# Hybrid MLA and sparse attention, two layers: scores ahead of the transposes of a step, a fourth buffer of probabilities, copies and exponentials by turns

## The reference

```python
h = rms_norm(x, attn_norm[l]); proj = h @ w_in[l]
o_mla = mla_attention(...)      # 8 heads, latent q and kv, rope, causal softmax, 4 query blocks of 128
o_nsa = nsa_attention(...)      # 8 heads, 2 kv groups: compressed + selected + window branches, gated
x = x + concat([o_mla, o_nsa]) @ w_out[l]
x = x + conv_ffn(rms_norm(x, ffn_norm[l]), ...)   # up projection, conv of width 3, silu gate, down projection
```

## Time and profile before

| what | value |
|---|---|
| median of 3 runs | 1303.52 us (1303.19 to 1304.73) |
| the profiled execution, own time | 1304.81 us |
| its span | 1303.0 us |
| PE / PEld / DVE / ACT busy over the span | 97% / 80% / 54% / 49% |
| granted TensorE clock, mean | 0.997 |
| share of the chain that ended last: PE / DVE / ACT | 84% / 8% / 6% |
| L1449 to L1451, matmul busy time of the costliest group of each | 298.2, 296.9 and 296.8 us |
| exponentials L860 | 192, 106.1 us busy, 28.5 us waited for `nmax` |
| transposes L1645 | 480, 72.1 us busy |

### The profile page before, as it was taken

One profiled execution on the slowest core, in us unless ns is written; L12 is line 12 of the kernel. 1 busy time (PEld: TensorE's weight loads), 2 busy tenths in 40 slices (PEclk: granted clock), 3 DMA queues, 4 the chain that ended last, 5 costly groups with the idle time before them and its releaser, 6 DMA issues.

```text
span 1303.0 us, 18497 instructions
## 1 busy us (share of the span) xinstructions
PE 1265.0 (97%) x6612; PEld 1045.6 (80%) x6612; DVE 704.0 (54%) x1232; ACT 639.2 (49%) x1193; POOL 71.1 (5%) x157
## 2 busy tenths in 40 slices
PE   8999989999999999999999998999999999999997
PEld 7997667778888888888889876677888888888885
DVE  5435887454555555533363459872555555554334
ACT  4336888344444444322352479881444444443223
POOL 2003020000000000000010311100000000000000
PEclk9999999999999999999999999999999999999999
DMA  6420200123333333332143211002233333333221
GB/s 206 125 90 1 98 34 1 39 73 113 95 93 100 95 93 102 103 97 96 53 122 95 65 66 50 17 1 81 81 85 95 97 97 95 96 101 108 97 64 65
DMA packets 121002, 107.04 MB, mean 82 GB/s; under 512 B 3763, under 2 KB 110485, under 8 KB 120946
## 3 DMA queue, kind: packets, MB, share of 16 engines
q1 hardware_dynamic: 118912, 101.13, 25.3%
q0 software_dynamic: 1456, 3.52, 0.9%
q10 hardware_dynamic: 578, 1.64, 0.3%
HBM read 104.19 MB, written 2.10 MB: 82 GB/s over the span
## 4 chain that ended last, share of the span: by engine, by line
PE 84%; DVE 8%; ACT 6%; issue 2%; DMA 0%; ACTq 0%; DVEq 0%
PE ps L1449 24%; PE ps L1451 24%; PE ps L1450 24%; PE ps L1692 3%; PE ps L1645 3%; DVE probs L1184 2%; ACT probs L860 2%; PE ps L1626 1%; PE ps L1632 1%; DVE w_lo L577 1%; PE ps L1631 1%; DVE probs L1057 1%; DVE x L1075 1%; PE ps L1704 1%; DVE ht_lo L1064 1%
## 5 line engine op out<-in xcount | busy, mean ns | idle before, releaser
L1449 PE MATMUL ps<-ht_hi,w_hi 128*128 128x512 f32 (+2 forms) x776 | 298.2, 384 | 2.5 <-DVE w_lo L577 2.5
L1450 PE MATMUL ps<-ht_lo,w_hi 128*128 128x512 f32 (+2 forms) x776 | 296.9, 383 | 0.0
L1451 PE MATMUL ps<-ht_hi,w_lo 128*128 128x512 f32 (+2 forms) x776 | 296.8, 382 | 0.0
L577 DVE TENSOR_TENSOR w_lo<-raw,w_hi 128x1024 fp32r<-128x1024 f32 (+4 forms) x196 | 219.8, 1146 | 96.0 <-ACT w_hi L570 86.9
L570 ACT ACTIVATE w_hi<-raw 128x1024 fp32r<-128x1024 f32 (+4 forms) x196 | 187.2, 983 | 108.0 <-PE ps L1451 107.1
L1365 DVE SCALAR_TENSOR_TENSOR conv<-ps,cols,conv 128x510 f32<-128x510 f32 (+1 forms) x176 | 127.6, 746 | 181.4 <-ACT conv L969 175.6
L1449 PEld LDWEIGHTS ps<-ht_hi,w_hi 128*128 128x128 f32 x776 | 146.4, 189 | 30.8 <-DVE w_lo L577 3.0
L1450 PEld LDWEIGHTS ps<-ht_lo,w_hi 128*128 128x128 f32 x776 | 146.5, 189 | 28.0 <-issue 0.5
L1451 PEld LDWEIGHTS ps<-ht_hi,w_lo 128*128 128x128 f32 x776 | 146.5, 189 | 27.8
L1449 PE MATMUL ps<-w_hi,ht_hi 128*128 128x430 f32 (+1 forms) x392 | 147.4, 376 | 2.6 <-DVE w_lo L577 1.5
L969 ACT ACTIVATE conv<-ps,cols 128x512 f32<-128x512 f32 x88 | 68.1, 773 | 160.0 <-PE ps L1451 159.8
(11 more groups left out here) (200 smaller groups left out, 1508.5 us busy)
## 6 DMA issues: line engine op xcount, KB each, us to landing
raw<-in_ffn_w_up_dram SPq DMA_DIRECT2D x88, 512.0 KB, 4.4
raw<-in_ffn_w_down_dram SPq DMA_DIRECT2D x44, 512.0 KB, 3.3
raw<-in_w_in_dram SPq DMA_DIRECT2D x32, 430.0 KB, 4.4
raw<-in_w_out_dram SPq DMA_DIRECT2D x16, 512.0 KB, 3.7
raw<-in_nsa_cmp_w_dram SPq DMA_DIRECT2D x8, 512.0 KB, 3.7
x<-in_x_dram ACTq DMA_DIRECT2D x3, 512.0 KB, 7.7
raw<-in_mla_w_uq_dram SPq DMA_DIRECT2D x4, 384.0 KB, 2.9
out_dram<-x SPq DMA_DIRECT2D x3, 512.0 KB, 2.6
```

What stands on the lines that cost most here:

```text
L577: last = nc.vector.tensor_tensor(d(w_lo)[:, :, d0:d1], r(raw)[:, :, r0:r1], d(w_hi)[:, :, d0:d1].bitcast(F32), ALU.subtract)
L1449: mm(o, lhs[0], rhs[0], start=start, stop=False)
L1450: mm(o, lhs[0], rhs[1], start=False, stop=False)
L1451: return mm(o, lhs[1], rhs[0], start=False, stop=stop)
```

## The change

PE: `scores(s)` now comes before `turn(s - 3)`. The order of a step is `spread`, `scores(s)`, `turn(s - 3)`, `values(s - 4)`, other jobs.

DVE: with `turn(s - 3)` behind `scores(s)`, `row_max(s)` may not write over the row of unit `s - 3`; so `probs` has four buffers instead of three, and `row_max(u)` waits for the transposes of unit `u - 4` instead of `u - 3`. The place comes from the second buffer of transposed rows, which only holds units of at most two blocks and is cut to half.

ACT: `evac_turn` becomes `evac_first` (head 0 of a big unit, or both heads of a small one) and `evac_second` (head 1 of a big unit), and `exps` becomes `exp_head`. The order is `evac_first(s - 3)`, exponential of head 0, `evac_second(s - 3)`, exponential of head 1.

```diff
-        probs = sb("probs", [P, 3, 2, S])
-        pts = [sb(f"probs_t{n}", [P, 2, T, 2 * P]) for n in range(2)]
+        probs = sb("probs", [P, 4, 2, S])
+        pts = [sb(f"probs_t{n}", [P, 2, T // (n + 1), 2 * P]) for n in range(2)]
...
                     if 0 <= s - T_LAG < U:
-                        evac_turn(s - T_LAG)
+                        evac_first(s - T_LAG)
                     if s < U:
-                        exps(s)
+                        exp_head(s, 0)
+                    if 0 <= s - T_LAG < U and big(s - T_LAG):
+                        evac_second(s - T_LAG)
+                    if s < U:
+                        exp_head(s, 1)
...
-                    if u >= 3:
-                        dve.wait_ge(t_done, at(t_done, l, turns(u - 3, 1 if big(u - 3) else 0)))
+                    if u >= 4:
+                        dve.wait_ge(t_done, at(t_done, l, turns(u - 4, 1 if big(u - 4) else 0)))
...
                 for s in range(U + LAG):
-                    if 0 <= s - T_LAG < U:
-                        if s == T_LAG:
-                            pe.wait_ge(q_ready, at(q_ready, l, H - 1))
-                        turn(s - T_LAG)
                     if s >= LAG and (s - LAG) % T == T - 1:
                         spread((s - LAG) // T)
...
                     if s < U:
                         scores(s)
+                    if 0 <= s - T_LAG < U:
+                        if s == T_LAG:
+                            pe.wait_ge(q_ready, at(q_ready, l, H - 1))
+                        turn(s - T_LAG)
```

More of the change, by code:

```diff
@@ L317, in hybrid_layers @@
         ffn.close()
-        kpe_r = pts[1][:, 0, :, 0:2 * ROPE].rearrange("p t (a b) -> p t a b", a=2)
+        kpe_r = pts[1].rearrange("p a t c -> p (a t) c")[:, :, 0:2 * ROPE].rearrange("p t (a b) -> p t a b", a=2)
         rows = pts[0][:, 0, :, :].rearrange("p a (b c) -> p (a b) c", c=P)
@@ L853, in _, with exp_head, evac_first @@
                     evac_proj(*job)
-                def exps(u):
+                def exp_head(u, h):
                     n = (unit(u)[0] + 1) * P
[L857 to L863, removed]
+                    row = probs[:, u % 4, h, 0:n]
+                    act.wait_ge(max_done, at(max_done, l, 2 * u + h + 1))
+                    activate(row, row, ACT.Exp, scale=-1.0, bias=nmax[:, u % 4, h:h + 1],
+                             accum_out=rsum[:, u // T % 2, unit(u)[0], h:h + 1]).then_inc(exp_done, 1)
+                def evac_first(u):
                     blocks, q = unit(u)[0] + 1, unit(u)[0] % 2 * P
@@ L872, in evac_turn @@
                                  ps[:, bank, 0:blocks * P].rearrange("p (b q) -> p b q", q=P), ACT.Copy).then_inc(pt_act, 1)
[L873 to L876, removed]
                     else:
@@ L880, in evac_turn, with evac_second @@
                             .then_inc(pt_act, 1)
+                def evac_second(u):
+                    blocks, q = unit(u)[0] + 1, unit(u)[0] % 2 * P
+                    act.wait_ge(t_done, at(t_done, l, turns(u, 1)))
+                    activate(pt_half(u)[:, 1, 0:blocks, q:q + P],
+                             ps[:, TURN_BANK[u, 1][0], 0:blocks * P].rearrange("p (b q) -> p b q", q=P), ACT.Copy)\
+                        .then_inc(pt_second, 1)
                 def evac_out(pair):
@@ L1179, in row_max @@
                     n = (unit(u)[0] + 1) * P
-                    if u >= 3:
-                        dve.wait_ge(t_done, at(t_done, l, turns(u - 3, 1 if big(u - 3) else 0)))
+                    if u >= 4:
+                        dve.wait_ge(t_done, at(t_done, l, turns(u - 4, 1 if big(u - 4) else 0)))
                     for h in range(2):
                         dve.wait_ge(sc_done, at(sc_done, l, 2 * u + (h + 1 if big(u) else 2)))
-                        v.tensor_tensor_reduce(probs[:, u % 3, h, 0:n], score_place(u, h), causal[:, S - n:S], -1.0, -NEG,
+                        v.tensor_tensor_reduce(probs[:, u % 4, h, 0:n], score_place(u, h), causal[:, S - n:S], -1.0, -NEG,
                                                ALU.add, ALU.min, nmax[:, u % 4, h:h + 1]).then_inc(max_done, 1)
@@ L1645, in turn @@
                             last = nc.tensor.transpose(ps[:, bank, c0 + b * P:c0 + (b + 1) * P],
-                                                       probs[:, u % 3, h, b * P:(b + 1) * P], ident[:, :])
+                                                       probs[:, u % 4, h, b * P:(b + 1) * P], ident[:, :])
                         if h == 1 or big(u):
```

## The result

| kernel | median | lowest to highest | profiled execution, span | granted clock, mean |
|---|---|---|---|---|
| before, beside it | 1304.12 us (8 runs) | 1303.14 to 1305.50 | 1304.81, 1303.0 us | 0.997 |
| after | 1307.70 us (8 runs) | 1306.99 to 1309.55 | 1307.5, 1305.7 us | 0.997 |

The ratio is 1.0026, interval 1.0017 to 1.0035: slower by 3.6 us. It is 2.3 us above the forecast and inside its range, but beyond the 0.2% that I called no change. A second comparison on another occasion gave 1307.47 against 1303.80 us, 1.0030 (1.0020 to 1.0039).

The account below looks back on a forecast made before the run. PE, busy 97%, bounds the kernel, but DVE and ACT take turns from 132.8 to 183.6 us. −2.25 + 0.25 + 1.75 + 1.2 = +0.95 a layer, +1.9 in two, gave 1305.4 us; range 1299.5 to 1310.5.

Parts of the forecast that it names:

- hidden layer earlier: Steps 5 and 7: scores moved ahead cover PE's waits for copies, so the hidden layer begins 2.25 us earlier a layer.
- still earlier at the first high part, 134.65: Step 8: scores ahead of transposes delay ACT's run, costing 0.25 us, so the lead falls from 2.25 to 2.0 us.
- V(21) of PE's half earlier: Values of step 25: gain of 2.25 less step 8's loss of 0.25, without ACT's turns, 2.0 us a layer.
- turns up to V(21): Steps 11, 12, 20, 23: ACT's second copy now follows its wait for DVE's maximum, +1.75 us a layer.
- groups: turns: PE-bound sparse-attention groups: values wait for the second copy, 0.30 us net in each of four, +1.2 us a layer.
- groups: PE's order: PE-bound sparse-attention groups: PE's new order, apart from the values' wait for the second copy, was given no cost.
- Gain: Steps 5 and 7: scores cover PE's waits for copies, gaining 1.24 us by step 5, 2.25 a layer in sum.
- A wait with a copy behind it: DVE-bound steps 11, 12, 20, 23: second copy slips behind the wait for the maximum, +1.75 us a layer, bounds 0 to 3.5.
- Values behind fewer scores: PE-bound sparse-attention groups: fewer scores cover the second copy, values wait 0.33 us, +1.2 a layer, bounds 0 to 3.6.
- turns cost nothing: Rival, attention stage: DVE leads enough that no exponential waits, −2.0 us a layer, 1299.5 us; faster had chance 0.23.
- V waits longer: Rival, PE-bound groups: ACT one exponential late, values wait 0.9 us, +3.35 a layer, 1310.2 us; both slower rivals together 0.37.
- The order does not do what it says: Rival, steps 5 and 7: transposes' bank is the wait, gain about 1.0, 1307.9 us; both slower rivals together 0.37.

Follow-up runs that it names:

- the clean pair: Kernel before and changed kernel, each with GpSimd's cast behind DVE's hidden-layer product and PE kept busy in the norm behind `w_out`: 1302.37 and 1304.49 us.
- PE's half: Changed kernel with ACT taking both copies before both exponentials: 1304.71 us; also with the later cast and PE kept busy in the norm: 1298.45 us.

## Why the prediction was right, and where it was short

Working in the order of its steps, with the clean pair as the measure (per layer):

| step | predicted | measured | from |
|---|---|---|---|
| hidden layer earlier | 2.25 | 2.20 | 26.06 to 23.86 |
| still earlier at the first high part, 134.65 | 2.0 | 1.70 | 33.46 to 31.76 |
| V(21) of PE's half earlier | 2.0 | 2.24 | 82.88 to 80.64 |
| turns up to V(21) | +1.75 | +1.74 | 80.64 to 82.38 |
| groups: turns | +1.2 | +1.22 | 62.29 to 63.51 |
| groups: PE's order | 0 | +0.31 | 61.98 to 62.29 |
| sum | +0.95 | +1.03 | 144.86 to 145.89 |

- **Gain.** Right in mechanism and size: S(5) and S(7) cover the wait for a copy. The first copy of the earlier trace rows was expected at 117.45 and came at 118.20, with the stage itself 0.65 us later; that is 0.1 off.
- **A wait with a copy behind it.** The sum was right to a hundredth, but not the places, so that hit is in part luck. Against PE's half, values of the changed kernel stood 0.10 us behind at V(11), 0.92 at V(13), 0.34 at V(15), 0.81 at V(19) and 1.74 at V(21): steps 11 and 12 left nothing at V(11), and half of the sum came in the last two steps. In step 12 ACT no longer waits for the maximum at all but 0.31 us for the transposes. V(21) is 0.50 us early, the "at most 0.5" of the prediction.
- **Values behind fewer scores.** The wait is there and a group takes 8.30 instead of 8.02 us (V at 92.22 and 100.52 in after, 92.26 and 100.28 before). That is the 0.27 us of the rows above, where I had 0.30. What I put at nothing, PE's own order in a group, costs 0.3 a layer; no run separates its scores from its factors.
- **Rival "turns cost nothing"** fell: they cost 3.0 us a layer (142.93 to 145.89). What the Trainium skill (Perfetto Trace Analysis, Optimizing Scalar/DVE Operations) says that breaking up instructions may do, let work be completed sooner, did not come about on this ACT. The pieces kept their length here and were only interleaved; what changed is that a copy now waits in order behind an operation that is not ready.
- **Rival "V waits longer"** fell for the changed kernel, and the second copy behind both exponentials shows it was one exponential away. **"The order does not do what it says"** fell with the hidden layer's start.
- **The step that was short is the last one, from the stages to the time.** I took all else as equal in both kernels. Of the 2.3 us between 1305.4 and 1307.7, 0.6 is the base, which was 1304.12 in the comparison and not 1303.52. 0.2 is the sum (2.1 instead of 1.9). The rest, 1.5, is put down to the two disturbances: taking them away brings the kernel before 1.43 us and the changed one 2.98 (1307.47 to 1304.49), each with about 1.2 us of uncertainty. Why they cost the changed kernel more is shown only in part. It isn't the late product by itself: by the ruler its removal takes 1.53 us from the two layers of before (145.65 and 145.62 to 144.86 and 144.88) and 1.07 from those of the changed kernel (145.99 and 146.86 to 145.89 twice). But behind a late product PE pauses 0.70 us in the kernel before and 1.81 in the changed one, and in two of the six profiles with that longer pause the clock fell at once. Both disturbances were in sight: the earlier trace rows gives a clock only for stretches of the stage, while at 290 us the profile of before has 0.75, and DVE's product stood at 1.18 us where its neighbours of the same size took 0.29.

## What to carry to other kernels

An in-order engine that fills its waits with copies is doing useful work in them: before interleaving two kinds of operation on it, count for each place what idles ahead of the operation that you move back, and add it up. Two halves of a change can have opposite signs, and here the half on PE was worth 3.9 us while the half on ACT, on top of it, cost 6.0. When a gain that the trace shows inside a stage is missing from the median, look at places where engines stand still only by a hair (a port shared with GpSimd, a pause of PE after which the clock falls), and remove them from both kernels before comparing.

## What the runs showed of the hardware that I had not expected

- A DVE product of 128 by 128 takes 0.29 or 1.17 us by whether it gets in at a seam between two GpSimd casts, with the same start to within 0.01 us (1.10 us after the first cast). It went one way in layer 0 and the other in layer 1 of the same execution, in seven profiles.
- A pause of PE of 0.96 and 1.47 us between weight loads was followed in some executions by a granted clock of 0.66 to 0.86 over 5 us, and in others of the same place by 1.00. With 15 transposes of the identity around it the clock was 1.00 there in all five profiles; elsewhere it could still fall, as to 0.77 and 0.83 over the 5 us from 1290 in two of them.
- The two can add up: a late product of 0.88 us made PE pause 1.81 us, and in one profile the clock of 0.52 behind it took another 1.63; in the first profile of the changed kernel the same pause was followed by a clock of 1.00.
